# An attention front with four banks, gate vectors stored by partition, and another order of the buffers

## The reference

```python
def post_norm_update(x, y, mod, j, g, b):
    gate = mod[:, 3 * j + 2][:, None, :]
    return layer_norm(ALPHA * x + gate * y, g, b)
```

```python
q, k, v = jnp.split(h @ w_qkv + b_qkv, [Q_WIDTH, Q_WIDTH + KV_WIDTH], axis=-1)
q = apply_axial_rope(q.reshape(B_, S_, N_HEADS, HEAD_DIM) * scale, cos, sin)
k = apply_axial_rope(k.reshape(B_, S_, N_KV_HEADS, HEAD_DIM), cos, sin)
kvc = hc @ w_qkv[:, Q_WIDTH:] + b_qkv[Q_WIDTH:]
```

## Time and profile before

| | before |
|---|---|
| median of the runs (lowest to highest) | 1677.95 us (1675.96 to 1678.39) |
| profiled execution | 1674.37 us |
| its span, and mean granted clock of TensorE | 1672.7 us, 0.989 |
| TensorE busy (matmuls) | 1596.4 us, 95% of the span |
| VectorE busy | 1200.0 us, 72% |
| ScalarE busy | 794.8 us, 48% |
| GpSimd busy | 140.3 us, 8% |
| moved by the DMA engines | 349.64 MB, mean 209 GB/s |

### The profile page before, as it was taken

One profiled execution on the slowest core, in us unless ns is written; L12 is line 12 of the kernel. 1 busy time (PEld: TensorE's weight loads), 2 busy tenths in 40 slices (PEclk: granted clock), 3 DMA queues, 4 the chain that ended last, 5 costly groups with the idle time before them and its releaser, 6 DMA issues.

```text
span 1672.7 us, 20900 instructions
## 1 busy us (share of the span) xinstructions
PE 1596.4 (95%) x7847; PEld 1318.7 (79%) x7847; DVE 1200.0 (72%) x1847; ACT 794.8 (48%) x1241; POOL 140.3 (8%) x205
## 2 busy tenths in 40 slices
PE   6999989999889999999999799999999999999997
PEld 6887768887778878888888458887888878888876
DVE  6888887987977776777756867777587775566544
ACT  4565534566434444444535465444354443264442
POOL 1100001100001110011100011111001110000000
PEclk9999999999999999999999999999999999999999
DMA  7864357753468877588658205987668866366552
GB/s 266 307 220 154 138 178 267 246 181 132 163 209 263 273 263 246 180 272 284 239 198 240 71 1 181 289 283 266 213 227 278 272 225 232 89 193 195 179 177 76
DMA packets 200509, 349.64 MB, mean 209 GB/s; under 512 B 11188, under 2 KB 128236, under 8 KB 199900
## 3 DMA queue, kind: packets, MB, share of 16 engines
q1 hardware_dynamic: 174668, 252.90, 46.5%
q0 software_dynamic: 25744, 95.43, 16.3%
HBM read 347.21 MB, written 1.08 MB: 208 GB/s over the span
## 4 chain that ended last, share of the span: by engine, by line
PE 82%; DVE 12%; ACT 2%; DMA 2%; issue 1%; SPq 0%; DVEq 0%; ACTq 0%
PE acc L579 24%; PE acc L581 24%; PE acc L580 24%; DVE w_lo L1488 3%; PE turn L923 1%; PE score L706 1%; DMA raw<-in_attn_wqkv 1%; PE acc L831 1%; PE score L1009 1%; DVE x L1589 1%; DVE att_work L2040 1%; DMA raw<-in_w_in 1%; DVE acc_ctx L1609 1%; PE score L718 1%; PE score L698 1%
## 5 line engine op out<-in xcount | busy, mean ns | idle before, releaser
L1488 DVE TENSOR_TENSOR w_lo<-raw,w_hi 128x1024 fp32r<-128x1024 f32 (+2 forms) x490 | 581.4, 1196 | 286.2 <-ACT w_hi L1124 285.2
L1124 ACT ACTIVATE w_hi<-raw 128x1024 fp32r<-128x1024 f32 (+2 forms) x490 | 503.5, 1040 | 505.1 <-PE acc L581 420.8
L579 PE MATMUL acc<-w_hi,xT_hi 128*128 128x512 f32 (+1 forms) x1440 | 573.0, 398 | 17.5 <-DVE wide L1738 6.6
L581 PE MATMUL acc<-w_hi,xT_lo 128*128 128x512 f32 (+1 forms) x1440 | 563.5, 391 | 0.0
L580 PE MATMUL acc<-w_lo,xT_hi 128*128 128x512 f32 (+1 forms) x1440 | 562.6, 391 | 0.0
L579 PEld LDWEIGHTS acc<-w_hi,xT_hi 128*128 128x128 f32 x1440 | 272.3, 189 | 74.0 <-issue 8.4
L581 PEld LDWEIGHTS acc<-w_hi,xT_lo 128*128 128x128 f32 x1440 | 272.2, 189 | 57.2
L580 PEld LDWEIGHTS acc<-w_lo,xT_hi 128*128 128x128 f32 x1440 | 272.5, 189 | 53.1
L479 POOL DMA_DIRECT2D mod_raw<-in_mod_w x144 | 104.3, 724 | 951.9 <-DVE mod_run L1609 758.3
L579 PE MATMUL acc<-w_hi,hT_hi 128*128 128x512 f32 x440 | 174.3, 396 | 0.1
L581 PE MATMUL acc<-w_hi,hT_lo 128*128 128x512 f32 x440 | 173.6, 395 | 0.0
(11 more groups left out here) (278 smaller groups left out, 1335.8 us busy)
## 6 DMA issues: line engine op xcount, KB each, us to landing
raw<-in_ffn_wi SPq DMA_DIRECT2D x220, 512.0 KB, 4.9
mod_raw<-in_mod_w POOLq DMA_DIRECT2D x144, 512.0 KB, 6.0
raw<-in_ffn_wo SPq DMA_DIRECT2D x110, 512.0 KB, 4.5
raw<-in_w_in SPq DMA_DIRECT2D x72, 512.0 KB, 7.2
raw<-in_w_out SPq DMA_DIRECT2D x16, 512.0 KB, 4.7
raw<-in_attn_wqkv SPq DMA_DIRECT2D x16, 512.0 KB, 4.7
wide<-in_b_merge POOLq DMA_DIRECT2D x4, 1024.0 KB, 10.1
raw<-in_w_branch_a SPq DMA_DIRECT2D x8, 512.0 KB, 4.6
```

Source lines behind the costliest of these rows:

```text
L579: nc.tensor.matmul(dst, xh, wh, start=start, stop=False)
L581: return nc.tensor.matmul(dst, xl, wh, start=False, stop=stop)
L1124: nc.scalar.activation(piece_part(w_hi[:, i % SPLIT_SLOTS, :], i), piece_part(raw[:, s, i % 2 * PIECE:(i % 2 + 1) * PIECE], i), ACT.Copy). ...
L1488: nc.vector.tensor_tensor(piece_part(w_lo[:, i % RAW_PIECES, :], i), piece_part(raw[:, i // 2 % RAW_SLOTS, i % 2 * PIECE:(i % 2 + 1) * PIE ...
```

## The change

- `gate_load` stores the vector by partition: element p of chunk k goes to place p * 8 + k. The row that is loaded back has this order, so the gate multiply reads it through a view with a step of 8 elements inside runs of 128, and gives its other operands by chunks of 128.
- The eight pairs of q and k are turned into four banks, `turn_bank(u % 4)`, in place of two; TensorE waits for the score banks too ahead of the first scores.
- GpSimd waits for the first `k_twice` ahead of `band`, and for the first exponentials ahead of the norm rows and, behind them, the gate.
- VectorE's splits move: the one ahead of the rotation of k goes behind the first `k_twice`; of the three that stood there, one goes behind the moves of the pairs and two into the last pair of heads, in place of the maxima that it no longer has.
- The buffers are allocated in another order: those of the first block and of the sublayers come ahead of x, the rings and the constants, in a room of fixed size; within the sublayers' room, the feed-forward and attention buffers come ahead of `ctx_area`, `gate_row`, `turned_more` and `gated`, and inside the attention's `qkv_bias` and `band` ahead of `qkv` and `ctx_kv`.

The diff, with the lines that only move an allocation left out:

```diff
+ROOM = 23600
...
         w_hi = sb("w_hi", [P, SPLIT_SLOTS, PIECE], F32R)
-        x = sb("x", [P, NT, D])
         xT_hi = sb("xT_hi", [P, KD, TOK], F32R)
         xT_lo = sb("xT_lo", [P, KD, TOK], F32R)
+
+        first = ExitStack()
+        scope[0] = first
+        cT_hi = sb("cT_hi", [P, 3, TOK], F32R)
...
+        first.close()
...
+        qkv_bias = sb("qkv_bias", [P, QKV])
+        band = sb("band", [P, NT, 2 * TOK])
+        qkv = sb("qkv", [P, NT, QKV])
+        ctx_kv = sb("ctx_kv", [P, NT, 2 * AKV * AD])
+        att_work = sb("att_work", [P, 8 * 512])
...
+        sb("ffn_room", [P, 2 * KF * TOK + 4 * NT * FC + MOD_KEPT * 512])
+        ctx_area = sb("ctx_area", [P, 2 * 2 * FHALF + NT * 3 * TOK + 12])
+        ctx_x = ctx_area[:, 0:NT * D].rearrange("p (t n) -> p t n", t=NT)
+        gate_row = sb("gate_row", [P, D])
+        turned_more = sb("turned_more", [P, 2, 512])
+        gated = sb("gated", [P, NT, D])
+        second.close()
+        scope[0] = ctx
+        sb("stage_room", [P, ROOM])
+
+        x = sb("x", [P, NT, D])
         mod_raw = sb("mod_raw", [P, MOD_RING, 2, 512])
...
@@ -493,7 +501,7 @@
                 n = c.now("gate")
                 v = (3 * j + 2) * KD
                 pool.wait_ge(mods_ready, stored)
-                pool.dma_start(gate_vectors[n].rearrange("(k p) -> p k", p=P), mod[:, v:v + KD], allow_slow_non_contiguous=True).then_inc(gate_out, 16)
+                pool.dma_start(gate_vectors[n].rearrange("(p k) -> p k", k=KD), mod[:, v:v + KD]).then_inc(gate_out, 16)
                 pool.wait_ge(gate_out, 16 * c.next("gate"))
                 pool.dma_start(gate_row[:], gate_vectors[n].partition_broadcast(P)).then_inc(gate_in, 16)
 
@@ -520,7 +528,9 @@
             gate_load(mod_ctx, 0, LAYERS)
             pool.wait_ge(ctx_ready, 2)
             pool.dma_start(qkv_bias[:], a["attn_bqkv_2"][0].partition_broadcast(P)).then_inc(att_in, 16)
+            pool.wait_ge(k_twice_ready, 1)
             pool.dma_start(band[:], a["band"].rearrange("(t p) n -> p t n", p=P)).then_inc(band_in, 16)
+            pool.wait_ge(exps_ready, 1)
             norm_rows(a["ln_g_2"][0, 1], a["ln_b_2"][0, 1])
             gate_load(mod_lat[:, 0, :], 1, LAYERS)
             for u in range(AH // 2):
@@ -982,9 +992,9 @@
                     project(ACC[0:2] if n % 2 == 0 else ACC[2:4], 4, after=after if n == 0 else None)
                 project(ACC[2:4], 4, after=ctx_turned, xh=ctxT_hi, xl=ctxT_lo)
 
-                def pairs(src):
-
-                    b = next_turn()
+                def pairs(u, src):
+
+                    b = turn_bank(u % 4)
                     dst = take(b)
                     for i in range(2):
                         for t in range(NT):
@@ -993,12 +1003,12 @@
 
                 pe.wait_ge(k_twice_ready, 1)
                 for u in range(4):
-                    pairs(lambda t, i: qkv[:, t, (2 * u + i) * P:(2 * u + i) * P + P])
+                    pairs(u, lambda t, i: qkv[:, t, (2 * u + i) * P:(2 * u + i) * P + P])
                 for kind in range(2):
                     pe.wait_ge(k_twice_ready, kind + 1)
                     for u in range(2):
-                        pairs(lambda t, i: k_twice[:, kind, t, 2 * u + i, :])
-                landed(*TURN)
+                        pairs(2 * kind + u, lambda t, i: k_twice[:, kind, t, 2 * u + i, :])
+                landed(*TURN, *SCORE)
 
                 def scores(u):
 
@@ -1893,7 +1903,9 @@
 
                 def gate(t, n):
                     at, b = slice(n * 512, n * 512 + 512), ACC[2 * n + t]
-                    nc.vector.scalar_tensor_tensor(out=gated[:, t, at], in0=bank[b][:], scalar=factor, in1=gate_row[:, at],
+                    by_chunk = lambda r: r.rearrange("q (k p) -> q k p", p=P)
+                    row = gate_row[:].rearrange("q (p k) -> q k p", k=KD)[:, 4 * n:4 * n + 4, :]
+                    nc.vector.scalar_tensor_tensor(out=by_chunk(gated[:, t, at]), in0=by_chunk(bank[b][:]), scalar=factor, in1=row,
                                                    op0=ALU.mult, op1=ALU.mult).then_inc(moved[b], 1)
 
                 def add(t, n):
@@ -2006,7 +2018,6 @@
                     for t in range(NT):
                         b = ACC[(0 if n % 2 == 0 else 2) + t]
                         nc.vector.tensor_tensor(qkv[:, t, n * 512:n * 512 + 512], bank[b][:], qkv_bias[:, n * 512:n * 512 + 512], ALU.add).then_inc(moved[b], 1)
-                split()
                 landed(*ACC[0:2])
                 for t in range(NT):
                     rotate_heads(t, AH, ROPED)
@@ -2014,7 +2025,7 @@
                     m = nc.vector.tensor_copy(k_twice[:, 0, t, :, :].rearrange("p h (i n) -> p h i n", i=2),
                                               qkv[:, t, AH * AD:ROPED * AD].rearrange("p (h n) -> p h n", n=AD).unsqueeze(2).to_broadcast([P, AKV, 2, AD]))
                 m.then_inc(k_twice_ready, 1)
-                split(3)
+                split()
 
                 products(4)
                 for t in range(NT):
@@ -2075,6 +2087,8 @@
                     inverse(2 * u + 1)
                     if u + 1 < AH // 2:
                         maxima(2 * u + 3)
+                    else:
+                        split(2)
                     if u:
                         scale_out(u - 1)
                     move_probs(u, 0)
```

More of the change, by code:

```diff
@@ new lines, in program @@
+        mod_sum_lat = sb("mod_sum_lat", [P, 512])
+        acc_ctx = sb("acc_ctx", [P, 2, 512])
+        first.close()
+        scope[0] = ctx
+        second = ExitStack()
+        scope[0] = second
+        ffn_scope = second.enter_context(ExitStack())
+        scope[0] = ffn_scope
+        hT_hi = sb("hT_hi", [P, KF, TOK], F32R)
+        hT_lo = sb("hT_lo", [P, KF, TOK], F32R)
+        silu_g = sb("silu_g", [P, 2, NT, FC])
+        hidden = sb("hidden", [P, 2, NT, FC])
+        mod_kept = sb("mod_kept", [P, MOD_KEPT, 512])
@@ new lines, in program @@
+        ffn_scope.close()
+        att_scope = second.enter_context(ExitStack())
+        scope[0] = att_scope
+        ctx_scope = att_scope.enter_context(ExitStack())
+        scope[0] = ctx_scope
+        ctxT_hi = sb("ctxT_hi", [P, KD, TOK], F32R)
+        ctxT_lo = sb("ctxT_lo", [P, KD, TOK], F32R)
+        ctx_scope.close()
+        scope[0] = att_scope
+        qT = sb("qT", [P, AH // 2, TOK])
+        kT = sb("kT", [P, AKV, 2 * TOK])
+        qkv_bias = sb("qkv_bias", [P, QKV])
+        band = sb("band", [P, NT, 2 * TOK])
```

90 lines of the change are left out of this document (28 added, 62 removed).

## The result

The changed kernel took 1665.8 us (median of 4 runs, 1662.2 to 1666.7) against 1677.7 for the kernel before beside it (4 runs): a ratio of 0.9927, 95% interval 0.9909 to 0.9944, 12 us less. The forecast was 1674.7 with a range of 1667.5 to 1680.5. The profiled execution took 1666.38 us, 8.0 less than the one of before (1674.4).

What follows compares the result with a forecast made beforehand. TensorE was taken to bound the kernel, with the chain on it for 82% of the span. The front's -10.3 and the gate multiplies' +7.1 summed to -3.2 us from 1677.95, forecasting 1674.7, range 1667.5 to 1680.5.

Steps and rivals of the forecast that it cites:

- Part 1: Front of the attention sublayer: weights arrive on time, splits move, four banks; first scores at 933.5, 10.3 us earlier.
- The band's price of nothing: Attention's first maximum: the later band load might stall VectorE by 0 to 1.1 us; taken as 0.
- the splits': VectorE's three splits taken out of the front come back in idle time of 1.35 and 2.66 us; cost nothing.
- The cause of the late load: Attention front: GpSimd's bias, band, norm rows and gate vector delay an attn_wqkv load; it lands after 15.2 us.
- Busy with small packets: Attention front, 901 to 905 us: full DMA engines moving 86 GB/s were taken to be filled by small packets.
- Part 2, the gate multiply: All 28 post-norm gate multiplies read one operand in steps of 8 elements and get longer; 7.1 us more in sum.
- The slot I took: Gate multiply: each stepped read takes one slot more, so a multiply of 512 grows by 0.54 us; chance 0.36.
- 12 d + 2 x (what 4 d has over 1.86): Post-norms: d is one gate multiply's growth; 12 count in feed-forward norms, the rest beyond idle time; 7.1 us.
- Other addresses ... Nothing: Reordered buffers: the rotation already worked at one element a slot, so new addresses were said to give nothing.
- the gate stores elsewhere: Gate stores outside the front: TensorE's only two waits for a split are the front's, so longer runs give nothing.
- the half-slot case: Rival, gate multiply: a step costs half a slot or less, up to 0.27 us a multiply; 1670.9; chance 0.28.
- The clock was foreseen only at the transposes: Attention's q transposes: 1.2 GHz was expected gone; if it stayed, the front gains 7.0 us, about 1678.

Runs made afterwards that it cites:

- e17_store: Kernel before with the gate vector's store by partition (32 bytes at a time) alone, the multiply staying unit-step: 1673.2 us, ratio 0.9981.
- e16_read: Kernel before with the gate multiply's stepped read alone, the store staying as it was: 1681.9 us, ratio 1.0034.
- e8_waits: Kernel before with GpSimd's two waits alone, so band, norm rows and gate store are issued later: 1671.7 us, ratio 0.9977.
- e12_banks: Kernel before with GpSimd's two waits and the four banks, splits where they were: 1670.4 us, ratio 0.9968.
- e5 to e7: Kernel before with hT up by 128 B: 0.9968; new buffer order alone with hT up by 896 B: 1.0002; the same order with xT at 172 KB: 0.9969.
- e9: Kernel before with all buffers up by 896 B, distances between them unchanged: 1674.1 us, ratio 0.9991.
- e10: Kernel before with hT and ctxT up by 512 B: 1677.1 us, ratio 0.9999.
- e13 to e15: Kernel before with weights up by 384 B and everything behind them by 512 B: 1.0070; with hT up by 384 B: 0.9963; with hT up by 192 B: 0.9999.
- e3_gate: Kernel before with both gate edits alone, the store by partition and the stepped multiply: 1678.6 us, ratio 1.0013.
- e2_front: Kernel before with the new attention front alone (GpSimd's two waits, moved splits, four banks): 1664.7 us, ratio 0.9925.
- e11_splits: Kernel before with GpSimd's two waits and the moved splits, without the four banks: 1668.2 us, ratio 0.9954.

## Why the prediction was right or wrong

- **What bounds the kernel, Part 1: right, step by step.** Forecast and profile after: piece 12 at 902.5 and 902.52, end of the first key copy 927.6 and 927.6, q transposes 928.9 and 928.5, scores 933.5 and 933.21. The band's price of nothing held, and so did the splits'. Measured alone, the part gave 12.6 us (10 to 15) where 10.3 was forecast.
- **The cause of the late load: right, but not shared out, and its picture was wrong.** I charged it to bias, band, norm rows and gate store together. e17_store shows that the store's 4-byte pieces by themselves were 6.7 of the 7.5 us. "Busy with small packets" was read into full engines that move 86 GB/s; what filled them were weight packets of 2 KB that took up to 4.2 us. I should have asked what the short store alone would do, since the change contains two cures for one fault.
- **Part 2, the gate multiply: right in kind, the term was mis-sized.** The slot I took was d = 0.54 us; measured 0.42 in the kernel after and 0.44 in e16_read. With the formula, 12 d + 2 x (what 4 d has over 1.86), that is 5.0 in place of 7.1, and e16_read measured 5.8 (3.7 to 7.7). The term left out the clock: behind the first of the three chains the longer multiplies bring a fall to 1.2 GHz, worth some 2 us in the kernel after. Per column the stepped read adds 0.42/512 = 0.82 ns to 1.33. The Trainium skill (Vector Engine (DVE) Microarchitecture Reference, section 5.2 Measured stream behaviour on trn2) led to estimates of 0.35 and 0.74; the measured value lies nearer the first. The section gives 2.50 ns, from which the second came, for steps of both sources or of the destination alone, not of one source.
- **Part 3, "Other addresses ... Nothing": this step failed.** It argued from VectorE's rotation, which runs at one element a slot wherever its operands lie, and said nothing of TensorE's operands, which bound the kernel. They gave 7.4 us (4.7 to 9.9): matmuls on hT at 391, 389 and 389 ns in place of 396, 395 and 395, by their distance from the weights. Without them the 1665.8 would have been some 1673, inside the range.
- **Part 3, the gate stores elsewhere: right.** e17_store gains 3.2 us in all, and its profile 2.6 of them between the context's norm and the attention's gate.
- **The sum.** -10.6 (front, profile), -7.5 (matmuls on hT) and +5.0 (gates) make -13.1; measured were -12 (9 to 15). With the failed step put right and nothing else, the forecast would have been 1667.2; with d too, 1665.1. Measured one by one, front, order and read make -12.6 - 7.4 + 5.8 = -14.2. The 2 us between this and the whole are within the intervals; whether the parts overlap isn't shown.
- **The rivals.** None happened. The nearest in size, the half-slot case of 1670.9, was the wrong cause. The clock was foreseen only at the transposes. That it would fall behind a feed-forward norm with longer multiplies was not, nor that closing only part of the front would be paid back through it (e8_waits, e12_banks); the latter did not touch the whole change.

What stays open: why the distance matters with a period of 256 bytes, and whether distances other than 0, 64 and 128 differ; by what means 4-byte pieces slow the weight packets beside them; and what decides in which executions TensorE's clock falls at the places where the profiles of like kernels differ.

## What to carry to other kernels

Before a reordering of buffers is put at nothing, compare the mean times of one instruction form over its operands: two groups of one shape that differ by 1% (here 395 against 391) on the engine that bounds the kernel are worth more than most rescheduling, here 5.4 us for 128 bytes of padding and 7.4 for the new order. Where a change carries two cures for one fault, price each alone: the short store and the later loads both freed the same weight load, and only the store brought a stepped read that cost 5 us. And a wait closed in part may be given back: TensorE idle for 2 us in one piece, then scores at half the clock.

## What the runs showed of the hardware

- A TensorE matmul of 128x512 in this fp32r product, with hT as stationary operand, takes 389 to 391 ns when stationary and moving operand lie a multiple of 256 bytes apart in the partition, and 394 to 397 ns at 64 or 128 bytes past one; the region of memory and a common shift do not matter (e5 to e7, e9, e10, e13 to e15).
- VectorE's multiply of 512 columns from PSUM with one SBUF operand in steps of 8 elements takes 1103 to 1120 ns against 684 to 686 with a contiguous one.
- A store of 1024 pieces of 4 bytes kept GpSimd 16.3 us and a 512 KB weight load, issued 2.6 us behind it, 15.2 us, with 2 KB weight packets of up to 4.2 us among 0.08 at the median; with 128 pieces of 32 bytes GpSimd waited 10.1 us at the same place and the load came 6.7 us earlier.
- In these profiles a stretch of 2.2 to 3.7 us of idle TensorE ahead of or between the attention's transposes was followed by 1.2 GHz (before, e3_gate, e8_waits, e12_banks, e16_read, e17_store); stretches of up to 1.04 us were not (after, e2_front, e11_splits).
